# The mask of sliding-window attention scores: added by VectorE in the bank instead of by a TensorE product

## The reference

```python
    s = jnp.einsum('bnqkgd,bnjkd->bnkgqj', qb, kb) * scale
    band = (diff >= 0) & (diff < SWA_WINDOW)
    s = jnp.where(mask, s, -jnp.inf)
    p = jax.nn.softmax(jnp.concatenate([s, sink], axis=-1), axis=-1)[..., :-1]
    o = jnp.einsum('bnkgqj,bnjkd->bnqkgd', p, vb)
```

## Time and profile before

| | |
|---|---|
| median of 3 runs | 2980.88 us (2980.04 to 3171.43) |
| the profiled execution | 2982.57 us; span 2981.0 us on core 5 |
| other cores' spans | 2970.1 to 2979.4 us |
| TensorE busy | 2865.3 us, 96% of the span |
| VectorE, ScalarE, GpSimd busy | 942.0, 776.5, 449.2 us |
| the two swa calls | about 501 to 621 us of the span |

### The profile page before, as it was taken

How to read it: one execution, slowest core, us unless ns; L and a number is a source line. 1 busy time by engine, 2 the same in 40 slices (tenths; PEclk the granted TensorE clock), 3 DMA queues, 4 the chain that set the end, 5 groups by cost and what they waited for, 6 DMA issues and landing times.

```text
span 2981.0 us, 39533 instructions; the slowest of 8 cores (2970.1 to 2981.0 us)
## 1 busy us (share of the span) xinstructions
PE 2865.3 (96%) x15292; PEld 1393.3 (47%) x15292; DVE 942.0 (32%) x1510; ACT 776.5 (26%) x1276; POOL 449.2 (15%) x597
## 2 busy tenths in 40 slices
PE   3899999999998999999999999999999999999997
PEld 1466444664444444444444444444444444444446
DVE  1434664455554476431111000000333101111015
ACT  2213454655554355331111000000211000111112
POOL 1010000000001565300000111111000000000222
PEclk9999999999999999999999999999999999999999
DMA  9966665335544334644444555555788544445844
GB/s 218 213 117 119 104 106 93 64 65 92 89 82 92 99 129 169 127 78 77 75 75 78 92 98 95 91 99 109 160 188 190 95 74 75 78 78 109 155 76 149
DMA packets 107032, 325.96 MB, mean 109 GB/s; under 512 B 11584, under 2 KB 28224, under 8 KB 100448
## 3 DMA queue, kind: packets, MB, share of 16 engines
q0 software_dynamic: 58320, 211.97, 44.2%
q1 hardware_dynamic: 48528, 111.46, 11.5%
HBM read 493.32 MB, written 42.01 MB: 180 GB/s over the span
## 4 chain that ended last, share of the span: by engine, by line
PE 86%; DVE 3%; DMA 3%; ACT 3%; issue 2%; POOL 2%; DVEq 0%; ACTq 0%; POOLq 0%; SPq 0%
PE bank L396 86%; DMA rmod<-wMA 3%; POOL acc L416 2%; DVE bank L416 1%; ACT rr L413 1%; ACT Pb L413 1%; ACT sq L413 1%; DMA cfb<-crow 0%; ACT qrot L413 0%; DVE sq L421 0%; DVE bank L421 0%; DVE Y L416 0%; ACT acc L413 0%; DVE y L416 0%; DMA rung<-wD 0%
## 5 line engine op out<-in xcount | busy, mean ns | idle before, releaser
L396 PE MATMUL bank<-mix,rung 128*128 128x512 bf16 x4096 | 885.0, 379 | 0.0
L396 PE MATMUL bank<-a,rung 128*128 128x512 bf16 (+1 forms) x4096 | 858.4, 372 | 1.7 <-DMA rung<-wD 1.7
L396 PEld LDWEIGHTS bank<-mix,rung 128*128 128x128 bf16 x4096 | 400.8, 98 | 484.3 <-issue 1.7
L396 PEld LDWEIGHTS bank<-a,rung 128*128 128x128 bf16 x4096 | 400.7, 98 | 458.4 <-issue 1.9
L396 PE MATMUL bank<-hT,ring 128*128 128x512 bf16 x1536 | 397.0, 382 | 1.7 <-DVE sq L421 1.3
L413 ACT ACTIVATE a<-bank 128x512 bf16<-128x512 f32 x256 | 152.8, 597 | 914.4 <-DVE bank L427 913.5
L427 DVE TENSOR_SCALAR bank<-bank 128x512 f32<-128x512 f32 x256 | 166.1, 695 | 647.1 <-PE bank L396 647.1
L413 ACT ACTIVATE Pb<-bank,Ctok 128x512 bf16<-128x512 f32 (+1 forms) x320 | 193.0, 623 | 268.2 <-DVE bank L416 265.6
L396 PE MATMUL bank<-mix,WO 128*128 128x512 bf16 x1024 | 234.1, 382 | 13.5 <-ACT sq L413 12.2
L416 POOL TENSOR_TENSOR acc<-acc,sq 128x512 f32<-128x512 f32 x172 | 215.8, 1267 | 187.5 <-ACT sq L413 182.5
L396 PEld LDWEIGHTS bank<-hT,ring 128*128 128x128 bf16 x1536 | 146.4, 98 | 155.8 <-issue 10.3
(11 more groups left out here) (145 smaller groups left out, 1765.7 us busy)
## 6 DMA issues: line engine op xcount, KB each, us to landing
rung<-wU POOLq DMA_DIRECT2D x128, 512.0 KB, 6.3
rung<-wD POOLq DMA_DIRECT2D x124, 512.0 KB, 6.3
ring<-wMB POOLq DMA_DIRECT2D x64, 512.0 KB, 6.7
ring<-wA POOLq DMA_DIRECT2D x34, 512.0 KB, 6.4
Y<-xP SPq DMA_DIRECT2D x16, 1024.0 KB, 6.1
x1s<-Y SPq DMA_DIRECT2D x16, 1024.0 KB, 3.9
xstA<-xP SPq DMA_DIRECT2D x8, 1024.0 KB, 15.9
rmod<-wMA POOLq DMA_DIRECT2D x16, 512.0 KB, 21.8
```

Source lines behind the costliest of these rows:

```text
L396: ins = e.matmul(o, lhsT=l, rhs=rh, start=st, stop=sp)
```

## The change

The mask is no longer part of the product. The score product closes its accumulation group alone, and a VectorE tensor_tensor adds the broadcast mask to the bank in place, behind it and ahead of ScalarE's Exp. It is issued in `sqk`, right after its product.

```diff
             m = mswa(slice(0, W))
             mb = m.re(m.ap.unsqueeze(1).broadcast_to([128, 2, W]))
-            pe([mm(ov, kk, q, True, False), mm(ov, ident(), mb, False, True)], [kk, q, ident(), m], [bk()])
+            pe([mm(ov, kk, q, True, True)], [kk, q], [bk()])
+            tt(ov, ov, mb, ALU.add)
             info[(kb, pair)] = (bk, W)
```

## The result

The changed kernel takes 2998.89 us in the median against 2980.88, 18.0 us more; the ratio is 1.0065 with a 95% interval of 1.0052 to 1.0078. So it is slower, by about 0.65%, which is less than 2%. Medians can hold runs in which one die was disturbed (the profiled execution of experiment e5 is one, and is read on core 0, of the other die), so the ratios compare undisturbed runs only.

What follows compares the result with a forecast made beforehand. TensorE was 96% busy, but a VectorE-ScalarE loop was to set the changed pace: calls +7.4 and +10.0, between them +1.2, start +0.6, sum +19.2 on 2980.9, plus about 1 for the clock: 3001 us, range 2998 to 3006.

Steps and rivals of the forecast that it cites:

- The loop: Sliding-window blocks: VectorE's queue closes into a loop with ScalarE, 4.03 us a block, 4.63 with a filler's copy.
- The sum over the calls: From first to last sink add of each sliding-window call: +7.4 us in the first, +10.0 in the second.
- TensorE's spare time: Each sliding-window block: TensorE stands still about 1 us, waiting for ScalarE to have read the score bank.
- The price of the add: VectorE's mask add in the score bank: holds the queue for 0.60 us, bounds 0.33 and 0.66.
- The ends: Outside the calls' steps: +0.6 us at the very start and +1.2 us between the two calls.
- Start +0.6: At the very start one add lies on the way to the first sink add: +0.6 us.
- The joint: Between the two sliding-window calls: two adds stand between block 15's norm product and the next first Exps, +1.2 us.
- Nothing gives it back: Stages behind the calls: nothing there recovers the +19.2 us; all that follows comes later by the same.
- The low clock inside the calls: Rival, chance 0.13: TensorE's clock falls in the calls; with 10 of 32 blocks cold, 3021 us.
- The saving that arrives: Rival, chance 0.07: the adds run in VectorE's 1.54 us hole, TensorE's 13.3 us come off, 2968 us.

Runs made afterwards that it cites:

- e5: Changed kernel without the adds; VectorE instead multiplies the bf16 tile Pb by zeros and ones behind ScalarE's Exp: 0.9959 of the kernel before, -12.2 us.
- e1: Changed kernel with the mask put in twice, by TensorE's identity product and by VectorE's add: 1.0066 of the kernel before, +19.7 us.
- e3: Changed kernel with the first pair's mask by TensorE's product again, the second pair's by VectorE's add: 1.0014 of the kernel before, +4.2 us.
- e4: Changed kernel with a block's two mask adds issued ahead of the previous block's norm product, not behind it: 0.9978 of the kernel before, -6.6 us.
- e7: e4 with the second call's first two scores and adds also issued ahead of the first call's last norm product: 0.9957 of the kernel before, -12.8 us.
- e2: Changed kernel without the adds, so no mask at all in the sliding-window scores: 0.9965 of the kernel before, -10.4 us.
- e6: Changed kernel with the filler tiles' copies in the two calls made by ScalarE in place of VectorE: 1.0044 of the kernel before, +13.1 us.

## Why the prediction was right

- **The loop.** Predicted 4.03 us and 4.63 with a copy; the changed trace has 4.03 and 4.63. The sum over the calls was +7.4 and +10.0, and came out +7.7 and +10.3; one step in each call is 0.28 longer, where the norm product comes late (549.90 to 552.41, 2.51 in place of 2.23). In the first call the time lies between ScalarE's Ln and Exp on that block's denominators, whose starts are 1.01 us apart (550.67 and 551.68) where they are 0.72 apart in the other blocks; why ScalarE paused there stays open. e1, e3 and e4 show the mechanism itself: the products on TensorE don't matter while the adds stand where they do, one add costs less than half of two, and moving the adds by one place in the queue turns the sign. TensorE's spare time in a block without a conditioning step is 4.03 - 3.04 = 0.99 us, the predicted 1 us; its records, in which a duration overlaps the next start, show less of it as a wait, (24.5 - 3.7) / 30 = 0.7 us a step in the mean.
- **The price of the add.** 694 ns and 0.60 us of the queue were taken from FoX's `cfb` add; the mask add has 690 ns and two take 1.29 us, so 0.60. The bf16 operand changes nothing. e5 has the counterpart: with both operands and the result bf16 outside the banks the instruction takes 416 ns, and two take 0.75. The Trainium skill, "VectorE: DVE Perf Modes", section "The perf-mode tier table", says that a tensor_tensor doubles its rate on bf16 in SBUF and stays at the single rate with a PSUM operand; the two measurements agree with it.
- **The ends.** Start +0.6: the first scores start at 501.06 and the sink add at 505.22 before, 498.98 and 503.76 after, so +0.6. The joint was put at +1.2, with 1 more for the clock on the slowest core; it is +2.8, and the low clock there came on every core of the changed kernel, not on the slowest alone. This term was 0.6 us too small, and the two adds are not what lengthens it. These are the first Exps of the second call in the kernel before and in the changed one:

```profile
561.00 1.06 ACT L413 ACTIVATE Pb<-bank 128x512 bf16<-128x512 f32 x2
568.85 1.20 ACT L413 ACTIVATE Pb<-bank 128x512 bf16<-128x512 f32 x2 [1.50 <-DVE bank L416]
```

That is 2.03 us behind the last sink add before and 3.61 after. Before, they follow ScalarE's norm directly; now they come behind the norm product (0.61 us until the next start) and the first add (0.78 until the Exp), +1.6 in place of +1.2, while the second add runs beside the first Exp.
- **Nothing gives it back.** The times agree with this step: the sum over the calls is +20.8 us, and the whole kernel's +19.4 has an interval of +15.5 to +23.3. The difference from the medians' 18.0 needs no cause. In the traces the MLP moved as a whole, as predicted, but two stretches in between did not, both by the clock. Behind the second call TensorE stands still for 3.54 us where it was 2.58 before, and then the clock falls on all eight cores where it fell on four before (0, 4, 5 and 6); on the other four it is 1.9 us more from the last sink add to the output projection. In the output projection those same four cores of the kernel before ran some products at the low clock, and no core of the changed kernel did. So the span grew by 21 to 25 us on cores 1, 2, 3 and 7, and by 13 to 16 us on the others. No term of the sum had these two parts, which come to +0.8 and -2.3 us in the mean over the cores. The forecast is borne out by the sums over the calls; that it also came within 2 us of the median of the whole kernel is in part luck.
- **The rivals.** The low clock inside the calls did not come, with up to 1.2 us of idle TensorE from one sink add to the next: 1.00 in the first call's window, and on no core of the changed kernel a fall between the first and the last sink add of either call. The section on psum-queue depth-cycling of the Trainium skill's "TensorE: Matmul & The Clock Gate" was thus not borne out in the calls; only the joint, with a wait of 3.7 us, and the stretch behind the second call show a fall. The saving that arrives was excluded by the order of the queue, and e4 and e7 bring most of it by changing that order alone. The argument for it was wrong on one point: the scores do not lie ready long before the hole; in e4 the adds wait 0.39 us for them and start 1.08 us behind the sink add. The advice of the Trainium skill, "Perfetto Trace Analysis", section "Identifying Performance Opportunities", to relieve the most-contended engine failed in the changed kernel and held in e2, e4, e5 and e7: TensorE's time counts only as long as no loop of other engines is longer.

## What to carry to other kernels

An engine that is 40% busy may still have no room: add up its queue between two instructions that wait for another engine, and see whether the new instruction falls into the wait or behind it. Here the same two adds in place of the products make the kernel 19 us slower behind the norm product and 7 us faster ahead of it, 13 with the joint in the same order. When work is moved off a saturated engine, write out the loop that it joins, and place it, in program order, where the receiving engine waits anyway.

## What the runs showed of the hardware

TensorE's standstill between the calls was followed by a lower granted clock (0.50, which is 1.2 GHz; in the changed kernel on core 4 from 570 to 572 us) on every core of the changed kernel, where it lasted 3.7 us, and on every core of e4 and e6 (3.2 and 3.1 us). In e1, also with 3.2 us, it was so on six of eight cores; in e3, with 1.7 us and soon after another 1.0, and in e5, with 1.7 us, on one of eight; in the kernel before (1.2 us), e2 (1.7 us) and e7 (1.6 us) on none. So the same standstill under the same program can be followed by the low clock on one core and not on another. Inside the calls of the changed kernel, where TensorE's longest idle stretch is 1.3 us, no core's clock fell. I hadn't expected that the low clock would be worth about 1.3 us at the joint, and 4.6 us in the output projection of the kernel before, where about 20 us were to be measured.
